# Mixing layer: the branch output products in tile pairs by Strassen's seven products

## What is computed

```python
y_lru = (gelu(gate_lru) * hl) @ w_lru_out        # [1024, 768] @ [768, 1024], recurrent branch
y_dil = o_dil @ w_dil_out                        # [1024, 256] @ [256, 1024], dilated attention branch
y_mem = om @ w_mem_out                           # [1024, 512] @ [512, 1024], memory attention branch
gt = sigmoid(gates + b_gate)                     # [1024, 3, 1024]
merged = gt[:, 0] * y_lru + gt[:, 1] * y_dil + gt[:, 2] * y_mem
x = x + merged @ w_out                           # x becomes the residual of the MLP
```

## Time and profile before

| | |
|---|---|
| time, three runs | 4018.42 us median (4014.6 to 4021.78) |
| the profiled execution's own time | 4013.84 us |
| span of the profiled execution | 4012.0 us, 48218 instructions |
| TensorE busy | 3926.0 us (98%) |
| VectorE, ScalarE, GpSimd busy | 1811.0, 954.8, 881.8 us |
| mean granted clock of TensorE | 0.991 of full speed |
| time of the branch products | from 2952.44 to 3118.22 us of the span |

### The profile page before, as it was taken

One profiled execution on the slowest core, in us unless ns is written; L12 is line 12 of the kernel. 1 busy time (PEld: TensorE's weight loads), 2 busy tenths in 40 slices (PEclk: granted clock), 3 DMA queues, 4 the chain that ended last, 5 costly groups with the idle time before them and its releaser, 6 DMA issues. The chain is left out here.

```text
span 4012.0 us, 48218 instructions
## 1 busy us (share of the span) xinstructions
PE 3926.0 (98%) x18442; PEld 2428.9 (61%) x18442; DVE 1811.0 (45%) x3807; ACT 954.8 (24%) x1802; POOL 881.8 (22%) x948
## 2 busy tenths in 40 slices
PE   7999999999999999989999999999999999999998
PEld 4688997776558468567544565656544444444447
DVE  3227775676343366646466322222533452223134
ACT  4223332333124311155225211111111010000000
POOL 0005774001111111133222112113100122122223
PEclk9999999999999999989999999999999999999999
DMA  5320003111211121132131112123253101111113
GB/s 214 129 89 10 8 9 68 42 47 53 84 58 46 50 64 51 55 112 93 48 98 63 51 39 69 42 69 106 82 186 105 53 32 42 43 50 44 42 44 104
DMA packets 113574, 270.26 MB, mean 67 GB/s; under 512 B 15480, under 2 KB 45034, under 8 KB 112255
## 3 DMA queue, kind: packets, MB, share of 16 engines
q1 hardware_dynamic: 106368, 251.81, 18.7%
q0 software_dynamic: 5920, 13.25, 1.3%
q10 hardware_dynamic: 1056, 2.10, 0.1%
HBM read 218.53 MB, written 50.87 MB: 67 GB/s over the span
## 5 line engine op out<-in xcount | busy, mean ns | idle before, releaser
L426 PE MATMUL upper_banks<-sbuf 128*128 128x512 f32 (+1 forms) x2016 | 771.2, 545 | 2.6 <-issue 2.1
L3210 PE MATMUL upper_banks<-sbuf 128*128 128x512 f32 x1400 | 613.5, 594 | 5.3 <-ACT sbuf L3490 3.5
L426 PEld LDWEIGHTS upper_banks<-sbuf 128*128 128x128 f32 x2016 | 382.5, 190 | 389.5 <-issue 373.8
L3210 PEld LDWEIGHTS upper_banks<-sbuf 128*128 128x128 f32 x1400 | 262.2, 191 | 315.5 <-issue 306.3
L2442 PE MATMUL gla_prod<-sbuf 128*128 128x512 f32 x560 | 247.5, 593 | 0.3 <-DVE sbuf L2474 0.3
L582 DVE TENSOR_TENSOR sbuf<-upper_banks,sbuf 128x512 f32<-128x512 f32 (+1 forms) x140 | 81.8, 584 | 284.0 <-PE upper_banks L426 283.5
L378 POOL TENSOR_TENSOR sbuf<-sbuf 128x512 f32<-128x512 f32 x36 | 47.2, 1312 | 660.3 <-DMA sbuf<-in_w_mlp_out 306.6
L2442 PEld LDWEIGHTS gla_prod<-sbuf 128*128 128x128 f32 x560 | 104.5, 192 | 119.9 <-issue 117.4
L1007 PE MATMUL mla_banks<-sbuf 128*128 128x128 f32 x1344 | 174.4, 278 | 2.4 <-DVE sbuf L1314 1.7
L1627 PE MATMUL mls_banks<-sbuf 128*128 128x512 f32 x392 | 175.1, 593 | 0.0
L1007 PEld LDWEIGHTS mla_banks<-sbuf 128*128 128x128 f32 x1344 | 162.1, 193 | 11.7 <-POOL sbuf L850 7.4
(11 more groups left out here) (558 smaller groups left out, 6574.0 us busy)
## 6 DMA issues: line engine op xcount, KB each, us to landing
sbuf<-in_l_w_in SPq DMA_DIRECT2D x59, 512.0 KB, 4.0
sbuf<-in_w_in SPq DMA_DIRECT2D x52, 512.0 KB, 4.2
sbuf<-in_w_mlp_out SPq DMA_DIRECT2D x40, 512.0 KB, 3.6
sbuf<-in_w_mlp_in SPq DMA_DIRECT2D x32, 512.0 KB, 3.5
sbuf<-in_l_w_mod SPq DMA_DIRECT2D x24, 512.0 KB, 5.0
scratch_gates<-sbuf SPq DMA_DIRECT2D x48, 256.0 KB, 2.0
sbuf<-scratch_gates SPq DMA_DIRECT2D x8, 1536.0 KB, 7.0
sbuf<-in_l_w_mod SPq DMA_DIRECT2D x8, 1024.0 KB, 15.4
```

What stands on the lines that cost most here:

```text
L426: last = nc.tensor.matmul(bank_of(n, c)[:, 0:wd], lw[:, k * P:(k + 1) * P], right_operand(c, base, tw, k, o, wd, to), start=k == 0 and c i ...
L3210: last = nc.tensor.matmul(pb, lw[:, k * P:(k + 1) * P], rhs, start=k == 0 and c in ("P1", "P2", "P5"), stop=k == 3, skip_group_check=True)
```

## The change

For each pair of output tiles p (4) and each branch (m memory, d dilated, l recurrent), the two tiles' products are made by the seven products of half depth: 2 matmuls a product for m, 1 for d, 3 for l. The order for a pair: the seven turns with m and d alternating, then the seven of l. The branches have banks of their own: m 0, 1, 2; d 6 and 7; l 3, 4, 5.

- Weights: `w_y` is stored anew so that two loads of 384 KB hold what m and d of a pair need, and two what l needs. The loads for the next pair are issued when this pair's m and d products (or l products) have ended.
- S sums: GpSimd makes four operations of 128x384 for m and d together, and four for l, for each pair.
- T sums: VectorE makes those of m and d once (12 operations of 128x512), GpSimd those of l (12 operations of 128x512, in `twist_recurrent` and `twist_recurrent_last`), which can start only when `yl` is back.
- Results: ScalarE copies out P1, P6 and P5 (`hold`), VectorE adds P2, P7 and P3 to those (`lift`), multiplies with the gate (`gate`), adds d to m (line 4108 of the new program) and l to that (line 4111), and then does `mix` as before.
- Transfers: the gates come in two parts for a pair (m and d 2 MB, l 1 MB); those of the first pair are issued ahead of `yl`. The residual is read back in two parts: rows 0 to 2 after the last pair's m and d products, the rest after its l products, since its place holds T sums until then.

```diff
+BR = []
+for p_ in range(4):
+    BR += [(p_, b_, c_) for c_ in TURNS for b_ in ("m", "d")] + [(p_, "l", c_) for c_ in TURNS]
+BR_DEPTH = {"m": 2, "d": 1, "l": 3}
+def branch_bank(b, c):
+    return {"m": (0, 1, 2), "d": (6, 7, 7), "l": (3, 4, 5)}[b][2 if c == "P2" else 1 if c in ("P5", "P3") else 0]
...
+        def holder(x):
+            p, b, c = x
+            i = KEEPS[c] if c in KEEPS else ADDS[c]
+            return corner(p, [e for e in ADDS if ADDS[e] == i][0]) if b == "m" else ev[:, i, :]
...
+            sp.wait_ge(scored, NS)
...
+            load_gates(0, 0)
+            load_gates(0, 1)
             evicted(sp, NCH)
             for o in (0, 512):
                 sp.dma_start(yl[:, :, o:o + 512], yv[:, :, o:o + 512]).then_inc(y_back, 16)
-            for j in range(2):
-                sp.dma_start(gy[:, j], gv[j]).then_inc(g_in[j], 16)
-            sp.dma_start(H[:, :, NCTX:T], hv).then_inc(h_back, 16)
...
+            for p in range(4):
+                t = NT + 4 * (p + 1)
+                load_w(t)
+                load_w(t + 1)
+                if p == 3:
+                    sp.dma_start(H[:, 0:3, NCTX:T], hv[:, 0:3, :]).then_inc(h_back, 16)
+                if p < 3:
+                    sp.wait_ge(paired, 4 * (p + 1))
+                    load_gates(p + 1, 0)
+                load_w(t + 2)
+                load_w(t + 3)
+                if p < 3:
+                    sp.wait_ge(merged, 4 * (p + 1))
+                    load_gates(p + 1, 1)
+            sp.dma_start(H[:, 3:KD, NCTX:T], hv[:, 3:KD, :]).then_inc(h_back2, 16)
...
+            branch_first(0, 0)
+            branch_first(0, 1)
+            branch_second(0, 0)
+            branch_third(0, 0)
+            twist_recurrent()
+            branch_second(0, 1)
+            twist_recurrent_last()
+            branch_third(0, 1)
+            for p in range(1, 4):
+                for n in range(2):
+                    branch_first(p, n)
+                    branch_second(p, n)
+                    branch_third(p, n)
...
+            def branch_product(x):
...
+                if prior is not None:
+                    if prior[2] in KEEPS:
+                        pe.wait_ge(held, BR_HELD[prior])
+                    elif prior[2] in ADDS:
+                        pe.wait_ge(lifted, BR_LIFTED[prior])
+                    else:
+                        pe.wait_ge(gated, BR_GATED[prior])
...
-            branch_products(0)
-            branch_products(1)
-            branch_recurrent(0)
-            branch_recurrent(1)
-            for n in range(2, 16):
-                branch_products(n)
-                branch_recurrent(n)
+            evicted(pe, NCH)
+            for e in BR:
+                branch_product(e)
...
+            for p in range(4):
+                for c in ("P1", "P6"):
+                    hold((p, "m", c))
+                    hold((p, "d", c))
+                if p == 0:
+                    gate_sigmoids(0, 0)
+                for b in ("m", "d"):
+                    hold((p, b, "P5"))
+                gate_sigmoids(p, 1)
+                for c in ("P1", "P6", "P5"):
+                    hold((p, "l", c))
+                if p < 3:
+                    gate_sigmoids(p + 1, 0)
...
+            for p in range(4):
+                for phase in (("m", "d"), ("l",)):
+                    todo = [(p, b, c) for c in TURNS if c in GIVES for b in phase]
+                    for i, e in enumerate(todo):
+                        lift(e)
+                        if i >= 2:
+                            gate(todo[i - 2])
+                    gate(todo[-2])
+                    gate(todo[-1])
```

More of the change, by code:

```diff
@@ L2973, in latent_block @@
         mixed, osummed = s.sem("mixed"), s.sem("osummed")
+        held, lifted, gated, paired, twist_md, twist_l, sum_md, sum_l = (
+            s.sem(c) for c in ("held", "lifted", "gated", "paired", "twist_md", "twist_l", "sum_md", "sum_l"))
+        h_back2 = s.sem("h_back2")
         od_out = [s.queue_sem(f"od_out{i}") for i in range(4)]
@@ L3050, in _, with load_gates @@
                     sp.dma_start(yv[:, i, :], av).then_inc(yl_out, 16)
+            gv = gates_dram.rearrange("(b j p) t -> j p b t", b=3, p=P)
+            def load_gates(p, n):
+                for a in range(2):
+                    b = slice(0, 1) if n else slice(1, 3)
+                    sp.dma_start(gy[:, a, b, :], gv[2 * p + a][:, b, :]).then_inc(g_in[n], 16)
+            sp.wait_ge(scored, NS)
+            early = max(ev_of[n] for n in gate_chunks if CH[n][2] <= 2 * KD) + 1
+            for e in range(NE):
+                sp.wait_ge(stored[e], 16 * sum(1 for i in range(early) if i % NE == e))
+            load_gates(0, 0)
+            load_gates(0, 1)
             evicted(sp, NCH)
@@ new lines, in twist_recurrent_last @@
+            def twist_recurrent_last():
+                pool.wait_ge(twist_l, 9)
+                for k in range(3):
+                    nc.gpsimd.tensor_tensor(B_t4["l"][k], half_of(yl, 3 + k, 0), B_t2["l"][k], ALU.subtract).then_inc(twist_l, 1)
+            pool.wait_ge(trans, NS)
+            branch_first(0, 0)
[5 more added lines that the diff above has]
+            twist_recurrent_last()
@@ L3156, in out_sums @@
+            branch_third(0, 1)
[4 more added lines that the diff above has]
+                    branch_third(p, n)
             def out_sums(p):
-                if p == 0:
-                    pool.wait_ge(trans, NS)
-                    pool.wait_ge(stored[2], 16 * sum(1 for i in ev_of.values() if i % NE == 2))
+                pool.wait_ge(yprod, BR_ENDS[3][0] + 1)
                 if p < 2:
@@ L3406, in branch_recurrent @@
-            def branch_recurrent(n):
-                j, half = divmod(n, 2)
-                t = NT + 2 * j
-                o = half * 512
-                if n < 2:
-                    pe.wait_ge(y_back, 32)
-                for k in range(6):
-                    last = nc.tensor.matmul(banks[:, 3 * (n % 2), :], w[:, t % NW, k * P:(k + 1) * P], yl[:, k, o:o + 512],
-                                            start=k == 0, stop=k == 5)
-                last.then_inc(yprod, 1)
-            branch_products(0)
@@ L3470, in _ @@
                 if n == 0:
-                    pe.wait_ge(merged, 15)
                     for b in range(2):
@@ L3924, in mix, with lift @@
                 nc.vector.tensor_tensor(xt4[k], pieces(lat[:, j, 0:512]), xt2[k], ALU.subtract).then_inc(mixed, 1)
[L3926 to L3939 removed]
+            def lift(x):
+                p, b, c = x
+                if c == "P4":
+                    return
+                dve.drain()
+                dve.wait_ge(yprod, BR_AT[x] + 1)
+                dve.wait_ge(held, BR_HELD[p, b, [e for e in KEEPS if KEEPS[e] == ADDS[c]][0]])
+                nc.vector.tensor_tensor(holder(x), banks[:, branch_bank(b, c), :], holder(x), ALU.add).then_inc(lifted, 1)
@@ new lines, in gate @@
+            def gate(x):
+                p, b, c = x
+                to = gate_of(p, b, c)
+                dve.drain()
+                dve.wait_ge(gate_sig, 6 * p + (6 if b == "l" else 4))
+                if c == "P4":
+                    dve.wait_ge(yprod, BR_AT[x] + 1)
+                nc.vector.tensor_tensor(to, banks[:, branch_bank(b, c), :] if c == "P4" else holder(x), to, ALU.mult).then_inc(gated, 1)
+                if b == "d":
+                    dve.drain()
+                    nc.vector.tensor_tensor(corner(p, c), gate_of(p, "m", c), to, ALU.add).then_inc(paired, 1)
+                if b == "l":
+                    dve.drain()
+                    nc.vector.tensor_tensor(corner(p, c), corner(p, c), to, ALU.add).then_inc(merged, 1)
+                    if c in ("P3", "P4"):
+                        mix(2 * p + (c == "P4"))
```

195 lines of the change are left out of this document (131 added, 64 removed).

## The result

The changed kernel took 4023.32 us, median of 21 runs (4016.62 to 4030.15), beside 4015.52 for the kernel before, median of 21 (4009.55 to 4022.43) on the same chip. The ratio is 1.0019 with a 95% interval of 1.0013 to 1.0025: 7.8 us slower. A second comparison gave 4021.76 beside 4017.31, 1.0012 (1.0003 to 1.0020). All runs of both kernels together, 32 against 87 over three comparisons, have means of 4022.6 and 4016.1: 6.4 us slower, and from their spread of 3.5 us that is uncertain by 1.5. The two comparisons that have the changed kernel differ by more than I can explain: 7.9 us in the means of one, 4.2 of the other. I had forecast 4018.0 and no change that can be measured.

The account below looks back on a forecast made before the run. TensorE, busy 98% of the span, was taken as the bound. Terms of -20.6, +8.6, +3.3, +5.1 and +3.2 gave -0.4 us: 4013.4 for the profiled execution, 4018.0 as median, range 4006 to 4028.

Parts of the forecast that it names:

- What goes: Branch products on TensorE: 192 matmuls become 168, 24 at 0.858 us fewer, 20.6 us less.
- The start: Before P6 of l in the first pair: TensorE waits for `yl` and GpSimd's sums, 8.6 us more (bounds 4.7 to 12).
- Pairs 1 and 2: VectorE's queue after l, before P5 of d: a wait of at most 0.5 us, taken as 0.
- Pair 3: Before P5 of d, behind VectorE's queue with six `mix` operations: a wait of 3.3 us (bounds 0.9 and 6).
- The end: P6 of the output product waits for VectorE's addition of P1, 13.7 us after the branch products: 5.1 more (bounds 2 to 6).
- The clock: TensorE at half clock after the idles before P6 of l and of the output, 1.6 us each: 3.2 us (bounds 0 and 6).
- Ends and small gaps: Extra semaphore waits in the stretch: nothing assumed, since 128 records of the output product keep the same pace.
- The sum: All terms together: -20.6 + 8.6 + 3.3 + 5.1 + 3.2 = -0.4 us.
- The faster rival: GpSimd and VectorE seldom meet, idles are shorter and the clock stays: -13 us, 4005 to 4006, partly so 4010; chance 0.28.
- The slower one: VectorE becomes the bound, with waits in pairs 1 and 2 and more in pair 3: 4026 us; chance 0.22.

Follow-up runs that it names:

- e4: Changed kernel with GpSimd's T sums of l and S sums of pairs 1 to 3 shrunk to one column (output wrong): 4009.06 us, before 4016.05.
- g2_start: Changed kernel with the first pair's l gates issued behind `yl` and P5 ahead of P6 in that pair's l: 4017.67 us, before 4015.14.
- e2: Changed kernel with pair 2's six mixing operations moved into pair 3, after the lift of P2 of d: 4016.89 us, before 4016.05.
- f4: Changed kernel with GpSimd's S sums of the output's second pair made only after the last mixing: 4015.14 us, before 4017.31.
- e1_yl_first: Changed kernel with the read-back of `yl` issued ahead of the first pair's gates: 4021.76 us, before 4016.05.
- e3_end: Changed kernel with f4's move, and VectorE adding the output's P1 ahead of the last gate's mixing: 4014.48 us, before 4016.05.
- f1_all: Changed kernel with e1_yl_first, e2 and e3_end together, and P5 copied before the sigmoids in the first pair: 4006.39 us, before 4017.31.
- g1_best: Changed kernel with the moves of g2_start, e2 and e3_end together: 4003.57 us, before 4015.14.

## Why the prediction was wrong

By its steps:

- **What goes.** Right: 336 records on one line, 0.429 us each, -20.6 us (forecast -20.6).
- **The start.** Right: `yl` reached GpSimd at 2980.3, 17.6 us after the first product, where the forecast had 16.5; the sums took 1.50 to 1.68 us each in the means of three (1.7), and the waits up to P6 of `l` are 8.9 us together (forecast 9.7, of which 1.1 were there before). That the cause is these sums is shown by e4. In g2_start `yl` reached GpSimd 15.7 us after the first product, 1.9 earlier, and the three matmuls of P5 ahead of P6 take 2.6; together that is nearly the 4.6 us by which the wait fell from 5.75 (it was 6.65 in the second profile).
- **Pairs 1 and 2.** Right: no wait.
- **Pair 3.** Right: 3.49 us (3.3). e2 shows the queue as the cause, e4 the share of the meetings, 2.0 (2.4), and of VectorE's own operations, 1.5 (0.9).
- **The end.** Right: P6 of the output starts 13.7 us after the first output product (13.7). f4 shows 2.7 us of it as meetings (3.3). Of before I had misread one row: the 0.39 us of the earlier trace rows are idle time of the weight loads, TensorE's products did not wait there; the 8.6 us hold without them.
- **The clock.** This is the step that failed. I wrote "3.2 us (bounds 0 and 6)", from two falls of 1.6 us; there were three, one of them behind the wait in pair 3 of which I said that it "stands between the two", and they cost 1.4, 2.7 and 1.6 us in one profile, 2.9, 1.7 and 3.0 in the other: 5.8 and 7.5 us. The 1.6 were read from a single fall. Falls differ: at that very place the second execution of the kernel before lost 3.1 us, nearly twice as much:

```profile
2103.14 6.68 PE L3210 MATMUL upper_banks<-sbuf 128*128 128x512 f32 x8 [3.95 <-ACT sbuf L3490]
```

  Behind the waits of the stretch it was 1.4 to 3.0 us. One case gave me the size, and the upper bound of 6 was reached in one profile and passed in the other. With 5.8 and 7.5 for 3.2 the sum is +2.2 and +3.9.
- **Ends and small gaps.** I had put them at nothing, since the output product with its waits keeps its pace. They are 1.6 and 1.8 us, and with them the sum is what the stretch shows, +3.5 and +5.6.
- **The sum.** The waits were forecast at 17.0 us together and measured at 16.7 and 16.9. They and 20.6 nearly cancel, so an error of 2.6 to 4.3 us in the term that I had sized least carefully, with the 1.6 to 1.8 that I had left out, gave the sign. (9 x 1.7 is 15.3, not 15.4, which changes nothing.)

The forecast took the kernel's time as no change, -0.4 us; the stretch says +4.5 in the mean of two profiles, the runs +6.4 ± 1.5. In absolute terms 2.9 us went the other way, since the kernel before has a median of 4015.5 in 21 runs where the three runs shown had 4018.4. The difference of 2 between stretch and runs stays open. One candidate is the late start that the last section describes. It adds 3 to 5 us to an execution, and five of the eleven profiles of the changed kernel and its variants have it, neither of the two of before. The spans hint that before has it too: of its executions with a mean clock of 0.992, 17 last 4008.5 to 4012.8 us and 14 last 4014.0 to 4017.2. A share of such executions that differs between two sets of runs would move their means by up to these 3 to 5 us, about as much as 7.9 and 4.2 lie apart. No run here shows the shares.

The faster rival was wrong, since the sums did meet VectorE's operations. The slower one was wrong in its main part, no wait came in pairs 1 and 2. That its 4026, or +7.8 us, is nearer to the result than my 4018 is luck; only its clock at half behind the wait in pair 3, which it had at 1.6 us, was right (2.7 and 1.7). In f4_pool_wait the same three operations take 0.69 us that take 1.58 beside GpSimd's sums. By the Trainium skill ("SBUF — State Buffer", Who interferes with whom) a VectorE operation with two inputs in SBUF contends with one of GpSimd that reads SBUF. The runs agree with it: 1.58 beside 0.69 us, and ends that alternate.

## What to carry to other kernels

When the bound engine's work is cut by moving sums to engines that were idle, the saving is paid out again at the few points where it now waits for them. Price each such wait with what the clock may take behind it, up to 3.1 us here behind waits of 3.1 and more, and read that price from several falls, not one. Then go for the order first: at none of the places here did anything have to be made faster, only to be queued behind what is wanted sooner (a sigmoid behind a copy, a mixing behind a lift, one load behind another).

## What was not expected of the hardware

- The same wait does not always lower the clock. Ahead of the stretch TensorE waits 3.11 to 3.15 us for VectorE in every execution. Of the thirteen, the clock stayed at 1.00 in four (before, e1_yl_first, e2_mix_later, e4_pool_small) and fell to 0.50 for 3 to 6 us in nine, with no edit near it. The clock 2 us behind it in the kernel before, and in its second execution:

```profile
2874.74:2876.74 2.00, 2.00 (x6) 1.00 0.04 15
```
```profile
2874.50:2876.50 2.00, 2.00 (x4) 0.50 0.04 14
```

It is so with longer ones: behind 3.49 us in pair 3 the 62 records take 29.56 us in the profile after, 28.4 to 29.6 in four others, but 26.88, full speed, in g2_start, with the same order of work there:

```profile
3084.27 26.88 PE L3530 MATMUL upper_banks<-sbuf 128*128 128x512 f32 x62 [3.49 <-DVE sbuf L4097]
```

So a wait of 3.1 to 3.5 us costs something between its own length and 3 us more; the waits of 2 us or less in the stretch (1.95 in g2_start, 1.79 in f4_pool_wait, 1.51 in e4_pool_small) did not lower the clock. What decides it, no run here shows. The forecast had taken one case of each, for what always happens.

- At the program's start the matmuls of the modulation ran at half speed until 31 us in one of thirteen executions (e3_end) and until 35 to 37 us in four (after, f4_pool_wait, f1_all, g1_best), and were twice as fast from 26 us on in the others. TensorE at that time, in the kernel before and after:

```profile
25.76 1.92 PE L216 MATMUL mod_acc<-sbuf 128*32 128x512 f32 x16
```
```profile
27.65 3.64 PE L216 MATMUL mod_acc<-sbuf 128*32 128x512 f32 x16
```

The granted clock of both reads 1.00 from 25 to 30 us, while in e3_end, where the same records take 3.64 us too, it reads 0.50; so the 1.00 of the row after is not to be trusted there. This late start moves the first layer's begin by 3 to 5 us (from 39.9 to 42.9 in e3_end and to 44.6 to 44.9 in the other four), in identical code. All five of those executions have the stretch begin at 2958.5 or later, the other eight at 2954.3 or earlier. Of the 10.2 us between the first two profiles, 5.0 stand at the start, 2.6 come before 2111 us and 2.7 behind the wait at 2873 and 2880 us, where the clock fell in the changed kernel's profile alone. With the late start and falls that come or not, much of the 13 us over which the runs of one kernel spread can be explained.
